# The output projection of a hybrid decoder block as seven half-size products behind the retention product

## The reference, cut to what matters

```
y_ret = (silu(g) * HeadNorm(Retention(...))) @ W_ret_o        # 2048 -> 1024
y_rnn = (RG_LRU(Conv(x_rnn)) * gelu(gate_rnn)) @ W_rnn_o      # 1024 -> 1024
mixed = sigmoid(m_ret) * y_ret + sigmoid(m_rnn) * y_rnn
x     = x + mixed @ W_out                                     # 1024 x 1024 x 1024
h     = RMSNorm(x)
x     = x + ConvGatedMLP(h)                                   # feed-forward
out   = RMSNorm(x)
```

## Time and profile before

| | |
|---|---|
| median of 3 runs | 1989.42 us (1987.3 to 1989.48) |
| profiled execution, first to last instruction | 1988.8 us |
| TensorE busy | 1961.3 us (99%) |
| VectorE, ScalarE, GpSimd busy | 1418.8, 934.4, 333.9 us |
| granted TensorE clock, mean | 0.998 of full speed |
| chain of waits, TensorE's share | 83% |
| chain of waits, VectorE's share | 9% |

### The profile page before, as it was taken

How to read it: one execution, slowest core, us unless ns; L and a number is a source line. 1 busy time by engine, 2 the same in 40 slices (tenths; PEclk the granted TensorE clock), 3 DMA queues, 4 the chain that set the end, 5 groups by cost and what they waited for, 6 DMA issues and landing times.

```text
span 1988.8 us, 24558 instructions
## 1 busy us (share of the span) xinstructions
PE 1961.3 (99%) x9208; PEld 1639.4 (82%) x9208; DVE 1418.8 (71%) x1621; ACT 934.4 (47%) x1182; POOL 333.9 (17%) x277
## 2 busy tenths in 40 slices
PE   8999999999999999999999999999999999999998
PEld 6888888888888888888888787997888888888887
DVE  7877876776755445667777658658987888776766
ACT  6443353343445555555555443346544544543335
POOL 2000010010392000067775003100000000000000
PEclk9999999999999999999999999999999999999999
DMA  6343554445697443465668555532222222256523
GB/s 259 117 169 137 180 181 157 169 158 179 206 327 281 159 159 127 148 200 173 206 190 256 199 196 194 184 112 84 85 91 78 84 84 84 74 191 234 199 96 132
DMA packets 222205, 325.07 MB, mean 163 GB/s; under 512 B 11824, under 2 KB 150448, under 8 KB 221872
## 3 DMA queue, kind: packets, MB, share of 16 engines
q1 hardware_dynamic: 196800, 232.84, 35.5%
q0 software_dynamic: 22608, 85.99, 11.0%
q10 hardware_dynamic: 2720, 5.24, 0.8%
HBM read 223.36 MB, written 100.66 MB: 163 GB/s over the span
## 4 chain that ended last, share of the span: by engine, by line
PE 83%; DVE 9%; ACT 3%; DMA 2%; issue 2%; POOL 1%; ACTq 0%; SPq 0%; DVEq 0%; POOLq 0%
PE ps L346 27%; PE ps L348 27%; PE ps L347 27%; DVE ws L329 1%; DMA stg<-scr_y 1%; DMA raw<-scr_q 1%; PE ps L1219 1%; POOL qkvs L949 1%; POOL state_s L955 1%; DVE ysr L2415 0%; DVE wx L2155 0%; POOL ws L968 0%; DVE wsr L2408 0%; ACT ri L1648 0%; DVE th L2337 0%
## 5 line engine op out<-in xcount | busy, mean ns | idle before, releaser
L1501 ACT ACTIVATE wx<-raw 128x1024 fp32r<-128x1024 f32 (+1 forms) x152 | 137.3, 905 | 252.3 <-DVE raw L2131 131.4
L346 PE MATMUL ps<-xs,wx 128*128 128x512 f32 x612 | 239.1, 391 | 2.1 <-DVE xs L2578 1.6
L348 PE MATMUL ps<-xs,wx 128*128 128x512 f32 x612 | 238.3, 389 | 0.0
L347 PE MATMUL ps<-xs,wx 128*128 128x512 f32 x612 | 238.2, 389 | 0.0
L2155 DVE TENSOR_TENSOR wx<-raw,wx 128x1024 fp32r<-128x1024 f32 (+1 forms) x152 | 158.9, 1047 | 30.4 <-ACT wx L1501 30.2
L346 PE MATMUL ps<-sc,wx 128*128 128x512 f32 x448 | 174.4, 389 | 0.0
L348 PE MATMUL ps<-sc,wx 128*128 128x512 f32 x448 | 174.3, 389 | 0.0
L347 PE MATMUL ps<-sc,wx 128*128 128x512 f32 x448 | 174.3, 389 | 0.0
L1536 ACT ACTIVATE ub<-ps 128x512 f32<-128x512 f32 x112 | 66.9, 597 | 159.1 <-PE ps L348 156.4
L346 PEld LDWEIGHTS ps<-xs,wx 128*128 128x128 f32 x612 | 114.9, 188 | 28.4 <-issue 2.7
L348 PEld LDWEIGHTS ps<-xs,wx 128*128 128x128 f32 x612 | 114.9, 188 | 24.1
(11 more groups left out here) (289 smaller groups left out, 4849.2 us busy)
## 6 DMA issues: line engine op xcount, KB each, us to landing
raw<-w_in SPq DMA_DIRECT2D x80, 512.0 KB, 5.5
scr<-ost POOLq DMA_DIRECT2D x32, 1024.0 KB, 5.2
raw<-w_up SPq DMA_DIRECT2D x44, 512.0 KB, 4.2
tq<-w_down SPq DMA_DIRECT2D x88, 128.0 KB, 2.7
scr_t<-tq POOLq DMA_DIRECT2D x22, 512.0 KB, 3.2
scr_h<-vt POOLq DMA_DIRECT2D x11, 1024.0 KB, 4.3
tr<-w_ret_o SPq DMA_DIRECT2D x64, 128.0 KB, 3.9
scr_q<-tr POOLq DMA_DIRECT2D x16, 512.0 KB, 5.2
```

What stands on the lines that cost most here:

```text
L346: pe.matmul(out, w(HI), x(HI), start=first, stop=False, skip_group_check=True)
L347: pe.matmul(out, w(HI), x(LO), start=False, stop=False, skip_group_check=True)
L348: return pe.matmul(out, w(LO), x(HI), start=False, stop=last, skip_group_check=True)
L1501: act.activation(dst, src, ACT.Copy).then_inc(sem["f_hi"], 1)
```

## The change

The projection `mixed @ W_out` becomes a seven-product scheme as well, in 14 chunks (`O_CHUNKS`) numbered 28 to 41, which follow the 28 of the retention product and use its buffers, splits and semaphores. A chunk has 24 matrix instructions of 512 columns. The order of products is `O_W`: quarter b11 of the weights with A11, b21 with A12, t2 with S2, t1 with S1 (in the place of A21), b22 with S4 (in the place of A12), t3 with S3 (in the place of A11), t4 with A22.

- The sums of quarters of `W_out` are formed in 8 pieces: SyncE loads them between the retention chunks 5 to 18 (`PIECES_AT`), GpSimd combines them after its last retention work and before the multiplications of the mixed rows, and stores them.
- The mixed rows stay float32 in the tile `mq`, five quarters. The 16 high and 16 low parts of rows go away; each chunk splits 2 tiles of a quarter instead (`out_y_hi`, `out_y_lo`).
- The sums of quarters of the rows are four on VectorE (`out_s3`, `out_s2`) and four on GpSimd, each 128 x 1024.
- VectorE adds to `x1` in blocks of 128 x 1024 (`out_add`), the last product in four of 128 x 512 (`out_last`).
- The first transposes stand in the middle of chunks 40 and 41, the second half's norms behind the last chunk.

In the cut below the lines stand in the order SyncE, GpSimd, TensorE, ScalarE, VectorE.

```diff
+O_CHUNKS = 14
...
+O_PIECES = 8
+O_W = ["b11", "b21", "t2", "t1", "b22", "t3", "t4"]
...
+O_FORM = [Q_A11, Q_A12, Q_S2, Q_A21, Q_A12, Q_A11, Q_A22]
...
+            def out_pieces(j):
+                k, cols, v = j // 2, j % 2 * BC, j % 4
+                if j == 0:
+                    sp_.wait_ge(sem["y_done"], 32)
+                sp_.wait_ge(sem[f"tr_out{v}"], 16 * ((R_PIECES + j) // 4))
+                for slot, r, n in ((0, 1, 1), (1, 0, 1), (2, 0, 0), (3, 1, 0)):
+                    row, col = (r * O_KT + k) * P, n * HALF + cols
+                    sp_.dma_start(tr[:, v, slot, :], w_o[row:row + P, col:col + BC]).then_inc(late_sem(f"tr_in{v}"), 16)
...
+            PIECES_AT = {5: (0,), 6: (1,), 7: (2,), 8: (3,), 11: (4,), 13: (5,), 17: (6,), 18: (7,)}
             for i in range(4, R_CHUNKS):
                 reto_w(i)
+                for j in PIECES_AT.get(i, ()):
+                    out_pieces(j)
...
+            for i in range(R_CHUNKS, R_CHUNKS + O_CHUNKS):
+                out_w(i)
+                if i == R_CHUNKS + 1:
+                    sp_.wait_ge(*late_count("ry_lo", R_CHUNKS))
+                    sp_.wait_ge(sem["x_re"], 16)
+                    sp_.dma_start(x1[:, 4:8, :], x_t[:, 4:8, :]).then_inc(sem["x_re"], 16)
+            sp_.wait_ge(*late_count("rw_lo", R_CHUNKS + O_CHUNKS))
+            load_up(1, 1)
...
+                k, cols, v, i = j // 2, j % 2 * BC, j % 4, R_PIECES + j
+                pool.wait_ge(*late_count(f"tr_in{v}", 64 * (i // 4 + 1)))
+                pool.tensor_tensor(tr[:, v, 0:2, :], tr[:, v, 0:2, :], tr[:, v, 1:3, :], ALU.subtract).then_inc(late_sem("tr_st"), 1)
...
+                pool.tensor_tensor(tr[:, v, 2, :], tr[:, v, 0, :], tr[:, v, 2, :], ALU.add).then_inc(late_sem("tr_st"), 1)
...
+                pool.tensor_tensor(tr[:, v, 3, :], tr[:, v, 3, :], tr[:, v, 2, :], ALU.subtract).then_inc(late_sem("tr_st"), 1)
...
+                pool.dma_start(scr_o[:, k * P:(k + 1) * P, cols:cols + BC].rearrange("q p c -> p q c"), tr[:, v, :, :]
+                               ).then_inc(sem[f"tr_out{v}"], 16)
...
+            for j in range(O_PIECES):
+                out_combine(j)
...
+            for c in range(2):
+                k = slice(2 * c, 2 * c + 2)
+                pool.wait_ge(sem["o_s"], 2 * c + 1)
+                pool.tensor_tensor(mq[:, Q_A21, k, :], mq[:, Q_A21, k, :], mq[:, Q_A22, k, :], ALU.add).then_inc(sem["o_p"], 1)
+            for c in range(2):
+                k = slice(2 * c, 2 * c + 2)
+                pool.wait_ge(sem["o_s"], 2 * c + 2)
+                pool.wait_ge(*late_count("ry_lo", R_CHUNKS + 2 + c + 1))
+                pool.tensor_tensor(mq[:, Q_A12, k, :], mq[:, Q_A12, k, :], mq[:, Q_S2, k, :], ALU.subtract).then_inc(sem["o_p"], 1)
...
+            def out_free(p, t):
+                if p == 0:
+                    pe.wait_ge(sem["acc"], 5 + t // 2)
+                elif p == 1:
+                    pe.wait_ge(sem["acc"], 7 + t)
+                else:
+                    pe.wait_ge(sem["x1_done"], (None, None, 1, 3, 7, 5, 11)[p] + t // 2)
...
+            def out(i, tiles=(0, 1, 2, 3)):
+                p, c, _ = out_at(i)
+                u = i % 2
+                pe.wait_ge(*late_count("rw_lo", i + 1))
+                pe.wait_ge(*late_count("ry_lo", i + 1))
+                for t in tiles:
+                    if c == 0:
+                        out_free(p, t)
+                    for k in range(2):
+                        last = mm3(pe, ps[:, O_BANK[p] + t, :], lambda q: ysr[u][:, q, k, t * P:(t + 1) * P],
+                                   lambda q: wsr[u][:, q, k, :], O_FIRST[p] and c == 0 and k == 0,
+                                   O_LAST[p] and c == 1 and k == 1)
...
+            for i in range(R_CHUNKS, R_CHUNKS + 12):
+                out(i)
+            out(R_CHUNKS + 12, (0, 1))
+            pe.wait_ge(sem["xn_done"], 8)
+            pe.wait_ge(sem["x1_done"], 10)
+            for k in range(4):
+                turn2(k, 0, k)
+            out(R_CHUNKS + 12, (2, 3))
+            out(R_CHUNKS + 13, (0, 1))
+            for k in range(4, 8):
+                pe.wait_ge(*late_count("a11_in", k - 3))
+                turn2(k, 0, k - 4)
...
+            def mixed_next(n):
                 act.wait_ge(sem["mx_f"], n + 1)
+                mix_load(act, n // 2 + 3)
+            def out_y_hi(i):
+                p, c, k = out_at(i)
+                u = i % 2
+                act.wait_ge(*((sem["mx_f"], 2 * c + 2), (sem["mx_f"], 6 + 2 * c), (sem["o_s"], 2 * c + 2), (sem["o_p"], c + 1),
+                              (sem["o_p"], c + 3), (sem["o_s"], 2 * c + 1), (sem["mx_f"], 10 + 2 * c))[p])
+                act.activation(ysr[u][:, HI, :, :], mq[:, O_FORM[p], k, :], ACT.Copy).then_inc(late_sem("ry_hi"), 1)
+            MIXED_NEXT = {23: 1, 24: 3, 26: 5, 27: 7}
...
+                if i in MIXED_NEXT:
+                    mixed_next(MIXED_NEXT[i])
...
+            for i in range(R_CHUNKS, R_CHUNKS + O_CHUNKS):
+                reto_w_hi(i)
+                out_y_hi(i)
+                if i == R_CHUNKS:
+                    mixed_next(9)
+                elif i == R_CHUNKS + 11:
+                    norm2(0)
+                    norm2(1)
+                elif i == R_CHUNKS + 12:
+                    norm2(2)
+                    norm2(3)
...
+            def out_s3(c):
+                k = slice(2 * c, 2 * c + 2)
+                dve.wait_ge(sem["mx_f"], 14 + 2 * c)
+                dve.wait_ge(*late_count("ry_lo", R_CHUNKS + c + 1))
+                dve.tensor_tensor(mq[:, Q_A11, k, :], mq[:, Q_A11, k, :], mq[:, Q_A21, k, :], ALU.subtract).then_inc(sem["o_s"], 1)
+            def out_s2(c):
+                k = slice(2 * c, 2 * c + 2)
+                dve.wait_ge(sem["o_s"], 2 * c + 1)
+                dve.tensor_tensor(mq[:, Q_S2, k, :], mq[:, Q_A22, k, :], mq[:, Q_A11, k, :], ALU.subtract).then_inc(sem["o_s"], 1)
...
+            i = R_CHUNKS
+            out_lo(i)
+            mixed(8)
+            mixed(9)
+            reto_last(0)
+            reto_last(1)
+            mixed(10)
+            mixed(11)
+            reto_last(2)
+            reto_last(3)
+            mixed(12)
+            mixed(13)
+            out_lo(i + 1)
+            mixed(14)
+            mixed(15)
...
+            out_lo(i + 2)
+            for c in range(2):
+                out_s3(c)
+                out_s2(c)
+            out_lo(i + 3)
+            out_add(0, 0, 0, 0)
+            out_add(0, 0, 0, 1)
+            out_lo(i + 4)
+            combine_t13(0, 0)
+            combine_t2(0, 0)
...
+            out_lo(i + 11)
+            norm2(0)
+            norm2(1)
+            out_add(5, 1, 1, 0)
+            out_lo(i + 12)
             norm2(2)
             norm2(3)
+            out_add(5, 1, 1, 1)
+            out_lo(i + 13)
             s_lo(A11, a11f, 0, 1)
             s_lo(A11, a11f, 1, 2)
+            prep_lo(0, 0, "b1")
+            combine_t4(0, 0)
+            out_last(0)
             s_lo(A12, a12f, 0, 3)
             s_lo(A12, a12f, 1, 4)
+            out_last(1)
+            norm2(4)
             prep_lo(0, 0, "t4")
             prep_lo(0, 0, "t2")
+            out_last(2)
             norm2(5)
+            out_last(3)
```

More of the change, by code:

```diff
@@ L1277, in turn2 @@
                 last.then_inc(sem["tr_ps"], 1)
[L1279 to L1307, removed]
@@ L1837, in _ @@
             s_hi(A11, a11f, lambda c: act.wait_ge(*late_count("a11_in", 2 * c + 2)))
+            for k in range(4):
+                turned(4 + k + 1)
+                act.activation(a12f[:, k, :], ps[:, k, :], ACT.Copy, scale=gcol[4 + k]).then_inc(late_sem("a12_in"), 1)
             act.wait_ge(sem["x1_st"], 32)
@@ L2533, in reto_last @@
                 dve.tensor_tensor(yacc[:, t, HALF:], yacc[:, t, HALF:], ps[:, t, :], ALU.add).then_inc(sem["acc"], 1)
-            mixed_lo(7)
-            mixed(8)
-            mixed(9)
-            split_lo(dve, *out_block(0))
-            mixed_lo(8)
-            mixed_lo(9)
-            for t in range(4):
-                reto_last(t)
-            mixed(10)
-            mixed(11)
-            mixed_lo(10)
-            split_lo(dve, *out_block(1))
-            mixed(12)
-            mixed_lo(11)
@@ new lines, in out_add, with out_last @@
+            def out_add(p, half, n, q):
+                dve.wait_ge(sem["o_ps"], 4 * p + 2 * q + 2)
+                dve.wait_ge(sem["x_re"], 16 * half + 16)
+                t, bank, cols = 4 * half + 2 * q, O_BANK[p] + 2 * q, slice(n * HALF, (n + 1) * HALF)
+                dve.tensor_tensor(x1[:, t:t + 2, cols], x1[:, t:t + 2, cols], ps[:, bank:bank + 2, :], ALU.add
+                                  ).then_inc(sem["x1_done"], 1)
+            def out_last(t):
+                p = len(O_W) - 1
+                dve.wait_ge(sem["o_ps"], 4 * p + t + 1)
+                dve.tensor_tensor(x1[:, 4 + t, 0:HALF], x1[:, 4 + t, 0:HALF], ps[:, O_BANK[p] + t, :], ALU.add
```

(28 more changed lines are left out.)

191 lines of the change are left out of this document (78 added, 113 removed).

## The result

| | before | changed |
|---|---|---|
| median, us | 1989.12 (4 runs) | 2007.01 (2006.49 to 2007.84, 4 runs) |
| profiled execution's span, us | 1988.8 | 2004.7 |
| granted TensorE clock, mean | 0.998 | 0.992 |

The changed kernel is slower: ratio 1.0089, 95% interval 1.0075 to 1.0104. That is 17.9 us between the medians and 15.9 between the two profiled spans. All that follows is counted in spans.

What follows compares the result with a forecast made beforehand. TensorE, 99% busy, was taken to set the pace almost everywhere. Nine terms, from -20.9 us of arithmetic to waits and slow clock, summed to +11.3: 1989.4 to 2000.7 us; range 1982 to 2009, the forecast's own 1995 to 2006.

Steps and rivals of the forecast that it cites:

- rival C: Chain is worse: pieces at 10 instead of 7, weights delayed at chunk 30, or a fourth slow start; 2007, chance 0.13.
- 1 arithmetic: Projection up to part(0,0,0): 79.7 us after instead of 100.6, -20.9 us if every chunk starts on time.
- 2 mixed stage: Chunks 23 to 27: high and low parts of rows leave, so some lost time returns; -2.0 us, bounds 0 and -4.06.
- 3 pieces: Chunks 5 to 8: GpSimd's piece operations and VectorE's exclude each other; +7.2 us, bounds 0 and 22.
- 4 chunk 28: High part of chunk 28's weights stands behind ScalarE's load issue, which waits for VectorE's row 7; +0.6 us (0 to 2).
- 5 chunk 29: VectorE must pass mixed(12) and mixed(13), needing the seventh pair's gate rows, before splitting chunk 29; +6.0 us, bounds 3 and 8.
- 6 chunk 31: VectorE's sums and low parts, with three GpSimd sums between, make chunk 31 late; +6.2 us, bounds 0 and 8.
- 7 chunk 40: VectorE's out_add(5, 1, 1, 0) stands ahead of chunk 40's splits and waits for chunk 39's end; +1.1 us (0 to 2).
- 8 tail: Waits of 3.0 at part(0,0,0), 0.5 at part(0,1,0), 5.6 at the second transposes; +9.1 us, bounds 3.5 and 11.
- 9 slow clock: Slow TensorE clock behind waits at chunks 29, 31 and the second transposes, 3 x 1.35; +4.0 us (0 to 6).
- rival B: At chunk 29 the gate rows land in time; 5 chunk 29 and its clock go, 7.4 us: 1993.3, chance 0.11.
- rival A: GpSimd fits VectorE's gaps in chunks 5 to 8 and 30; 14.8 us go: 1985.9, chance 0.17.

Runs made afterwards that it cites:

- e4: Changed kernel with SyncE issuing x1's second half behind the weights of chunk 31 instead of chunk 29; span 1999.4 us, median 2000.91.
- e12: Changed kernel with two edits: VectorE splits chunk 29 ahead of mixed(12), x1's second half loads behind chunk 31's weights; span 2001.2 us, median 2003.31.
- e2: Changed kernel without GpSimd's three operations per piece (sums then wrong), loads and stores kept; span 1997.7 us, median 1999.88.
- e8: Changed kernel with GpSimd's four 128x1024 sums made by VectorE in chunks 32 to 35; span 1997.8 us, median 1999.62.
- e10: Changed kernel with VectorE making the pieces' sums, with chunks 9 to 12, 14, 15, 19 and 20; span 1999.6 us, median 2000.37.
- e3: Changed kernel with VectorE splitting chunk 29 before mixed(12) instead of behind mixed(13); span 2002.3 us, median 2004.49.
- e5: Changed kernel with VectorE splitting chunk 31 between the two pairs of sums (out_s3, out_s2) instead of behind both; span 2002.1 us, median 2003.76.
- e6: Changed kernel with only the order of ScalarE's and VectorE's work behind the last splits changed; span 1995.8 us, median 1998.29.

## Why the prediction was right, and where it was off

The forecast was slower, 2000.7 us, by +11.3; measured is +15.9 in span, +17.9 in time. That is inside the range of 1982 to 2009, but above the forecast's own 1995 to 2006: 2007.01 is rival C's 2007.

| step | forecast | measured | from |
|---|---|---|---|
| 1 arithmetic | -20.9 | -20.9 | 106.1 us from chunk 27 to part(0,0,0) before, 109.9 after, less 24.6 of waits and slow clock |
| 2 mixed stage | -2.0 | -2.1 | chunks 22 to 27: 31.26 before, 29.15 after |
| 3 pieces | +7.2 | +5.2 | chunks 4 to 22: 103.56 for 98.18, less 0.2 by which chunk 4 began earlier |
| 4 chunk 28 | +0.6 | +0.6 | |
| 5 chunk 29 | +6.0 | +11.0 | 16.44 from its predecessor's start |
| 6 chunk 31 | +6.2 | +3.4 | |
| 7 chunk 40 | +1.1 | +1.1 | |
| 8 tail | +9.1 | +7.6 | 2.8 + 0 + 4.8 |
| 9 slow clock | +4.0 | +10.0 | 2.9 + 2.8 + 1.7 + 2.6 |

The places and signs of the nine steps were right, the runs bear out the mechanism of steps 3 and 5 to 8, and the clocks in the windows that of step 9; steps 2 and 4 had no run of their own. Sizes were off in both directions: steps 5 and 9 were 11.0 us too small together, steps 3, 6 and 8 were 6.3 too large. That the sum came out within 4.6 us is in part luck.

*Step 5* is one of the two most mis-sized ones. The rows landed 14.3 us after chunk 27's start (1242.5) where 11.0 was reckoned: from the issue at 1244.0 on, 4.4 MB went in 12.8 us, where 3.7 MB in 10 had been reckoned. From there to chunk 29's first instruction 8.2 us passed where 6.6 was reckoned: one port wait was counted, three came. What the step did not see at all is what e4 and e12 show: with the loads in time the chunk still waits, because VectorE's own work and its turns with GpSimd are too long. So rival B was wrong in its price: it had 7.4 us for timely rows, and the run that made them timely gained 5.3, of which 3.1 were waits at chunks 29 to 31 and some 2 less slow clock. (The 9.29 us that rival B quotes are GpSimd's idle time; the pair was used 10.0 us after its issue.)

*Step 9* is the other. It took 1.35 us per slow start, from 15 instructions of 256 columns. Here, at chunks 29 and 31, 14 of 512 columns were slow, at 0.43 instead of 0.23 us, 2.8 us each; and the wait at part(0,0,0) brought a fourth, which stood in the bounds as an aside.

*Steps 3 and 6* were 2.0 and 2.8 too large. For step 3 the turns between the engines cost 2.5, 1.2 and 1.2 us instead of 2.8, 1.9 and 2.3. For step 6 the chain was as long as reckoned (1268.4 to 1282.0, 13.6 us against 13.9), but it began 3.4 us after chunk 29's start instead of 4.7, and chunks 29 and 30, with the longer slow start, covered 13.8 us instead of 12.4.

*Rival A* is refuted by e2, e8 and e10: GpSimd's arithmetic is what holds VectorE, and taking it away removes the waits. *Rival C* has the number, but only one of its three causes: the fourth slow start, 1.7 us. The pieces came in under their price (5.2, not 10), and TensorE did not wait at chunk 30.

*The turns between queues.* From 1244.5 to 1247.5 us, right behind the issue at 1244.00, and from 1247.5 to 1250.5 and 1250.5 to 1253.5 (q1 is SyncE's queue, q10 ScalarE's; columns: packets, MB, share):

```profile
q1 hardware_dynamic: 231, 0.94, 84.5%
q10 hardware_dynamic: 7, 0.01, 1.7%
...
q1 hardware_dynamic: 159, 0.65, 63.1%
q10 hardware_dynamic: 150, 0.31, 32.3%
...
q1 hardware_dynamic: 242, 0.70, 59.7%
q10 hardware_dynamic: 245, 0.47, 41.8%
```

ScalarE's queue gets nearly nothing for some 3 us behind its issue, and from 1247.5 us on as many packets as SyncE's, which are the larger ones. The Trainium skill, page "DMA: Bandwidth & Descriptors", section "Queues, rings and completion order", says that a DMA engine takes turns between queues, packet by packet. From 1247.5 to 1253.5 the trace agrees, 395 packets beside 401; before that ScalarE's queue is hardly served. The prediction set the rule aside by a window that ends at 1246, 3.4 us behind the issue; in the trace of before, too, the packets are equal right after it (133 beside 131 from 1246.5 to 1248.5). It did not help the estimate made by the rule: the loads came 3.3 us later than the forecast had them, not 1.5 earlier.

## What to carry to other kernels

A scheme that saves an eighth of the products pays only if the extra additions have an engine to stand on. Count, stage by stage, the time of GpSimd and of VectorE's operations with two SBUF operands as one sum; where it exceeds TensorE's time, moving an operation to GpSimd makes it dearer (2.35 for 1.14 us), and reordering, in e3, e5 and e12, mostly handed the wait on. Price a wait of some us with a slow start behind it, by the columns of what follows, and allow for its staying away. And before counting a late load as the cause, ask what would be late if it came in time.

## What the runs showed of the hardware

A slow start was not tied to one length of wait. Up to chunk 5 the changed kernel and e4 are the same program, and in their profiled executions chunk 5 waited 2.35 and 2.31 us; behind it the granted clock was 1.00 in the one and 0.65 in the other (windows from chunk 5's start, columns as above):

```profile
1117.80:1121.20 3.40, 3.37 (x15) 2.81 (x16) 3.40 (x3) 0.00 (x0) 2.85 (x3) 1.00 0.90 312
```

```profile
1117.30:1120.70 3.40, 3.36 (x10) 2.73 (x11) 3.40 (x3) 0.00 (x0) 2.84 (x3) 0.65 0.90 312
```

There it cost nothing, as chunks 6 and 7 wait for VectorE anyway: chunk 7 starts 13.4 us after chunk 5 in both. At chunk 31 it did. The changed kernel waited 3.4 us there and ran behind it at 0.50; e6 waited 3.7 us, and its chunk 31 ran at full clock, 2.7 us shorter:

```profile
1283.20:1288.80 5.60, 5.49 (x24) 4.57 (x25) 5.60 (x5) 0.00 (x0) 2.41 (x1) 1.00 0.13 38
```

Where a slow start came, the price went with the instructions that fell into it: 24 transposes at 0.21 instead of 0.11 us cost 2.6, 14 instructions of 512 columns 2.8. So a single execution can carry 2.7 us more or less for one long wait, which the spans above should be read with. And an operation of GpSimd that waits for VectorE is recorded with its waiting time (3.43 for 2.38), as VectorE's is (3.42 for 1.21), so the busy time in a summary is too high there.
